# Layer 1 of a two-layer trunk: attention of each head interleaved with the input projection of the next

## What is computed

```python
def _diff_attn(q, k, v, lam):
    ...
        s = jnp.einsum("bqhmd,bnhmd->bhmqn", qi, k2).astype(jnp.float32) * scale
        p = jax.nn.softmax(s, axis=-1)
        amap = p[:, :, 0] - lam * p[:, :, 1]
        return jnp.einsum("bhqn,bnhe->bqhe", amap.astype(v.dtype), v)

def _mixer_c(h, j, l, W, rope, cache):
    q, k, v = jnp.split(h @ W["w_in_c"][j], 3, axis=-1)
    ...
        keys = jnp.concatenate([k_ctx, _rope_pairs(k, rope)], axis=1)
        vals = jnp.concatenate([v_ctx, v], axis=1)
        o = _diff_attn(_rope_pairs(q, rope), keys, vals, lam)
    of = o.astype(jnp.float32)
    of = of * lax.rsqrt(jnp.mean(of * of, axis=-1, keepdims=True) + SUBLN_EPS) * W["c_subln"][j] * (1.0 - lam_init)
    out = of.astype(h.dtype).reshape(bn, t, C_HEADS * C_VDIM) @ W["w_out_c"][j]
    return out, (k, v)
```

## Time and profile before

| | us |
|---|---|
| median of 3 runs | 4068.52 |
| span of the profiled execution | 4070.0 |
| layer 1, input projection (2917.6 to 3089.3) | 171.7 |
| layer 1, attention (3089.3 to 3488.5) | 399.2 |
| layer 1, output projection (3488.5 to 3547.1) | 58.6 |

### The profile page before, as it was taken

One profiled execution on the slowest core, in us unless ns is written; L12 is line 12 of the kernel. 1 busy time (PEld: TensorE's weight loads), 2 busy tenths in 40 slices (PEclk: granted clock), 3 DMA queues, 4 the chain that ended last, 5 costly groups with the idle time before them and its releaser, 6 DMA issues.

```text
span 4070.0 us, 55614 instructions
## 1 busy us (share of the span) xinstructions
PE 3540.9 (87%) x22346; PEld 3286.8 (81%) x22346; DVE 1839.3 (45%) x2902; ACT 998.3 (25%) x1729; POOL 0.2 (0%) x4
## 2 busy tenths in 40 slices
PE   7899998875979797978999989999897555799998
PEld 7899998854868686868999989999895222699997
DVE  2554545443454544445545455554413555332223
ACT  1212122232121212122121232112323444232212
POOL 0000000000000000000000000000000000000000
PEclk6899999965877776879999999999998666899999
DMA  6344441100000000022444424343220000122221
GB/s 193 89 119 119 119 115 56 29 0 19 1 4 1 4 1 2 1 58 60 121 114 114 124 83 117 106 127 110 78 72 7 5 5 25 52 64 81 72 73 57
DMA packets 393639, 264.46 MB, mean 65 GB/s; under 512 B 11627, under 2 KB 375430, under 8 KB 393222
## 3 DMA queue, kind: packets, MB, share of 16 engines
q1 hardware_dynamic: 393478, 262.23, 22.8%
HBM read 258.13 MB, written 4.06 MB: 64 GB/s over the span
## 4 chain that ended last, share of the span: by engine, by line
PE 83%; DVE 10%; ACT 3%; issue 3%; DMA 1%; SPq 0%; DVEq 0%; ACTq 0%
PE pair L1960 56%; PE pair L761 5%; PE pair L1946 2%; PE pair L1274 1%; PE pair L1969 1%; PE pair L1926 1%; DVE big L1780 1%; PE pair L721 1%; PE pair L799 1%; PE pair L722 1%; PE pair L756 1%; PE pair L802 1%; PE pair L1269 1%; DVE w_lo_as_f L1383 1%; PE pair L421 1%
## 5 line engine op out<-in xcount | busy, mean ns | idle before, releaser
L1960 PE MATMUL pair<-h_hi,w_hi 128*128 128x320 f32 x3792 | 875.7, 312 | 120.3 <-DVE h_lo L1789 68.1
L1960 PE MATMUL pair<-h_lo,w_hi 128*128 128x320 f32 x3792 | 873.1, 312 | 0.0
L1960 PE MATMUL pair<-h_hi,w_lo 128*128 128x320 f32 x3792 | 872.3, 312 | 0.0
L1960 PEld LDWEIGHTS pair<-h_hi,w_hi 128*128 128x128 f32 x3792 | 642.1, 190 | 124.1 <-issue 124.1
L1960 PEld LDWEIGHTS pair<-h_lo,w_hi 128*128 128x128 f32 x3792 | 642.8, 190 | 0.0
L1960 PEld LDWEIGHTS pair<-h_hi,w_lo 128*128 128x128 f32 x3792 | 641.7, 190 | 0.0
L1960 PE MATMUL pair<-big_as_f32r,w_hi 128*128 128x320 f32 x2816 | 538.8, 314 | 4.6 <-DVE w_lo L1679 4.4
L1569 ACT ACTIVATE w_hi<-raw 128x1024 fp32r<-128x1024 f32 x333 | 341.3, 1052 | 630.9 <-PE pair L1960 333.0
L1679 DVE TENSOR_TENSOR w_lo<-raw,w_hi 128x1024 fp32r<-128x1024 f32 x333 | 397.5, 1216 | 163.5 <-ACT w_hi L1569 162.7
L1960 PEld LDWEIGHTS pair<-big_as_f32r,w_hi 128*128 128x128 f32 x2816 | 451.3, 192 | 5.6 <-DVE w_lo L1679 5.2
L1824 DVE TENSOR_TENSOR work<-work,pair 128x640 f32<-128x640 f32 x88 | 72.2, 821 | 644.0 <-PE pair L1960 644.0
(11 more groups left out here) (345 smaller groups left out, 3571.1 us busy)
## 6 DMA issues: line engine op xcount, KB each, us to landing
raw<-ffn_w SPq DMA_DIRECT2D x272, 512.0 KB, 5.0
work<-mod_w SPq DMA_DIRECT2D x136, 512.0 KB, 3.8
raw<-w_in_c SPq DMA_DIRECT2D x24, 512.0 KB, 3.8
raw<-w_in_ab SPq DMA_DIRECT2D x21, 512.0 KB, 3.9
w_hi_as_f<-mod_w SPq DMA_DIRECT2D x8, 512.0 KB, 4.7
raw<-w_out_ab SPq DMA_DIRECT2D x8, 512.0 KB, 5.4
raw<-w_out_c SPq DMA_DIRECT2D x8, 512.0 KB, 5.1
h_hi_as_f<-x_sample SPq DMA_DIRECT2D x1, 2048.0 KB
```

Source lines behind the costliest of these rows:

```text
L1960: ins = nc.tensor.matmul(ps[:, c, 0:HALF], w, v[:, k, c * HALF:(c + 1) * HALF], start=(k == 0 and w is hi and v is xh), stop=(k == kts - 1 ...
```

## The change

Projection and attention of layer 1 become one hand-ordered stage, written out head by head without a loop. The columns of the weight matrix are taken head by head (queries, keys, values of head 0, then of head 1, and so on). Three tiles are projected ahead; then PE runs, for each head, the steps of its attention with the three projection tiles of the next head between them, each in two halves. The weighing and the mean squares of a head run inside the next head. All projection tiles go through one PSUM pair (3); scores of the two halves take pairs 0 and 1, one block at a time; everything else (rotations, transposes, keys, values, weighing, mean squares) takes pair 2. The scratch of the attention moves to `big` behind the tiles of two heads, to `work` and to a part of `attn`, so the weight rings and the projection's input stay in use. Maxima, exponentials and sums run over 640 keys in one instruction instead of 512 and 128; the prompt's 128 keys go with block 0. The transfers of cached keys and values and of the prompt's rows go from SP's queue to POOL's. The last head splits the finished output tiles between its own steps, and the weight splits run ahead into the output projection.

The core of the diff (the helpers of ACT and DVE not shown keep their operations):

```diff
-            return i + 1 < len(stages) and stages[i + 1][0] != "out"
+            return i + 1 < len(stages) and stages[i + 1][:2] != ("out", 0)
...
+        def c_tile(h, kind):
+            return big[:, 8 + 3 * (h % 2) + kind, :]
+        CB = 14 * TOK
+        c_keys, c_q = R[:, CB:CB + 640], R[:, CB + 640:CB + 1152]
+        c_vtok = R[:, CB + 1152:CB + 1792].rearrange("p (c n) -> p c n", n=P)
+        c_t2 = R[:, CB + 1792:CB + 2816].rearrange("p (a n) -> p a n", a=2)
+        c_o, c_sq, c_rs = (R[:, CB + 2816 + 640 * i:CB + 3456 + 640 * i] for i in range(3))
+        c_kout, c_kpast, c_vpast, c_ap = (R[:, CB + 4736 + P * i:CB + 4736 + P * (i + 1)] for i in range(4))
...
+        c_e = work[:, 0:2560].rearrange("p (q m n) -> p q m n", q=2, m=2)
+        c_at = work[:, 2560:5120].rearrange("p (i n) -> p i n", i=5)
+        c_a = [attn[:, 1664:2304], work[:, 5248:5888]]
+        C_SPARE, C_PROJ = 2, 3
...
+        def pool_attn_c(pool):
+            kc, vc = T["cache_c_k"][0, 0], T["cache_c_v"][0, 0]
+            pool.wait_ge(n_lo, DT * norm_before["in", 1, 0, 0] + DT)
             for i, name in enumerate(("c_lq1", "c_lq2", "c_lk1", "c_lk2")):
+                pool.dma_start(c_lq[:, i, :], T[name].to_broadcast([P, HD])).then_inc(c_lam, 16)
+            pool.dma_start(c_kpast, kc[:, 0, :]).then_inc(c_load, 16)
+            def keys_out(h):
+                pool.wait_ge(c_act, CAC.value(f"kt_{h}"))
+                pool.dma_start(T["new_c_k"][0, 0][:, h, :], c_kout).then_inc(c_outk, 16)
+                if h + 1 < CH:
+                    pool.dma_start(c_kpast, kc[:, h + 1, :]).then_inc(c_load, 16)
+            keys_out(0)
+            for h in range(CH):
+                if h:
+                    pool.wait_ge(c_pe, CPE.value(f"pv_{h - 1}"))
+                pool.dma_start(c_vpast, vc[:, h, :]).then_inc(c_loadv, 16)
+                if h + 1 < CH:
+                    keys_out(h + 1)
+                pool.wait_ge(c_act, CAC.value(f"vt_{h}"))
+                pool.dma_start(T["new_c_v"][0, 0][:, h, :], c_vtok[:, 4, :]).then_inc(c_outv, 16)
...
+        def pe_attn_c(pe, products):
...
+            def project(j, first=True, last=True):
+                if first:
+                    pe.wait_ge(lo_full, IN_C + j + 1 + RING)
+                    pe.wait_ge(pair_free, IN_C + j + RING)
+                for k in range(0 if first else DT // 2, DT if last else DT // 2):
+                    if j == 0:
+                        pe.wait_ge(n_lo, DT * norm_before["in", 1, 0, 0] + k + 1)
+                    ins = products(pp[C_PROJ], (IN_C + j) % RING, k, h_hi, h_lo, k == 0, k == DT - 1)
+                if last:
+                    ins.then_inc(slab_used, 1)
...
+            def scores(h, b):
+                if b == 0:
+                    pe.wait_ge(c_dve, CDV.value(f"r2_{h}"))
+                    pe.wait_ge(c_act, CAC.value(f"kt_{h}"))
+                    if h:
+                        pe.wait_ge(c_act, CAC.value(f"ex3_{h - 1}"))
+                else:
+                    pe.wait_ge(c_act, CAC.value(f"ex{b - 1}_{h}"))
+                for k0, k1 in ((0, 512), (512, 640)):
+                    for m in range(2):
+                        r = slice(m * HD, m * HD + HD)
+                        ins = nc.tensor.matmul(flat[m][:, k0:k1], c_q[r, b * P:(b + 1) * P], c_keys[r, k0:k1], start=True, stop=True)
+                if b == 0:
+                    for m in range(2):
+                        r = slice(m * HD, m * HD + HD)
+                        ins = nc.tensor.matmul(flat[m][:, 640:768], c_tile(h, 0)[r, LAT:TOK], c_tile(h, 1)[r, LAT:TOK],
+                                               start=True, stop=True)
+                ins.then_inc(CPE.sem(f"sc{b}_{h}"), 1)
+            def turn(h, b):
+                pe.wait_ge(c_dve, CDV.value(f"A{b}_{h}"))
+                if b == 0 and h:
+                    pe.wait_ge(c_act, CAC.value(f"o_{h - 1}"))
+                elif b == 1:
+                    pe.wait_ge(c_act, CAC.value(f"rt_{h - 1}" if h else f"at0_{h}"))
+                elif b == 2:
+                    pe.wait_ge(c_act, CAC.value(f"vt_{h}"))
+                elif b == 3:
+                    pe.wait_ge(c_act, CAC.value(f"at2_{h}"))
+                if b == 0:
+                    nc.tensor.transpose(flat[C_SPARE][:, 640:768], c_ap, ident)
+                for i in range(5):
+                    ins = nc.tensor.transpose(flat[C_SPARE][:, i * P:(i + 1) * P], c_a[b % 2][:, i * P:(i + 1) * P], ident)
+                ins.then_inc(CPE.sem(f"tr{b}_{h}"), 1)
...
+            for j in range(3):
+                project(j)
+            rotate(0)
+            turn_keys(0)
+            scores(0, 0)
+            for h in range(CH):
+                more = h + 1 < CH
+                j = 3 * h + 3
+                if more:
+                    project(j, last=False)
+                if h:
+                    turn(h - 1, 3)
+                if more:
+                    project(j, first=False)
+                if h:
+                    weigh(h - 1)
+                scores(h, 1)
+                turn(h, 0)
+                if more:
+                    project(j + 1, last=False)
+                if h:
+                    mean_squares(h - 1)
+                if more:
+                    project(j + 1, first=False)
+                scores(h, 2)
+                turn(h, 1)
+                if more:
+                    project(j + 2, last=False)
+                    rotate(h + 1)
+                scores(h, 3)
+                if more:
+                    project(j + 2, first=False)
+                    turn_keys(h + 1)
+                turn_values(h)
+                if more:
+                    scores(h + 1, 0)
+                turn(h, 2)
+            turn(CH - 1, 3)
+            weigh(CH - 1)
+            mean_squares(CH - 1)
...
+        def act_attn_c(act, split_hi):
...
+            keys(0)
+            for h in range(CH):
+                more = h + 1 < CH
+                j = 3 * h + 3
+                exps(h, 0)
+                if more:
+                    split_hi(0, IN_C + j + 2)
+                if h:
+                    turned(h - 1, 3)
+                if more:
+                    evict(j)
+                if h:
+                    outputs(h - 1)
+                turned(h, 0)
+                exps(h, 1)
+                if more:
+                    split_hi(0, IN_C + j + 3)
+                if h:
+                    roots(h - 1)
+                if more:
+                    evict(j + 1)
+                else:
+                    split(0)
+                    split(1)
+                turned(h, 1)
+                exps(h, 2)
+                if more:
+                    split_hi(0, IN_C + j + 4)
+                else:
+                    split(2)
+                    split(3)
+                exps(h, 3)
+                if more:
+                    evict(j + 2)
+                    keys(h + 1)
+                values(h)
+                turned(h, 2)
+            split(4)
+            split(5)
+            turned(CH - 1, 3)
+            outputs(CH - 1)
+            split(6)
+            roots(CH - 1)
+            act.wait_ge(c_outk, 16 * CH)
+            act.wait_ge(c_outv, 16 * CH)
+            split(7)
...
+        def dve_attn_c(dve, split_lo):
...
+            def mapped(h, b):
+                u = c_unit(b)
+                parts = [(c_e[:, b % 2], b + 1, c_a[b % 2])] + ([(c_ep, 0, c_ap)] if b == 0 else [])
+                dve.wait_ge(c_act, CAC.value(f"ex{b}_{h}"))
+                v.reciprocal(c_rd[:, u, :], c_den[:, u, :]).then_inc(CDV.sem(f"rd{b}_{h}"), 1)
+                own(f"rd{b}_{h}")
+                v.tensor_scalar(c_l1[:, u, :], c_rd[:, u, 1:2], nlam, None, ALU.mult).then_inc(CDV.sem(f"lm{b}_{h}"), 1)
+                own(f"lm{b}_{h}")
+                for e, i, _ in parts:
+                    ins = v.tensor_scalar(e[:, 1, :], e[:, 1, :], c_l1[:, i, :], None, ALU.mult)
+                ins.then_inc(CDV.sem(f"tm{b}_{h}"), 1)
+                own(f"tm{b}_{h}")
+                if b == 0 and h:
+                    dve.wait_ge(c_pe, CPE.value(f"tr2_{h - 1}"))
+                for e, i, out in parts:
+                    ins = v.scalar_tensor_tensor(out=out, in0=e[:, 0, :], scalar=c_rd[:, i, 0:1], in1=e[:, 1, :],
+                                                 op0=ALU.mult, op1=ALU.add)
+                ins.then_inc(CDV.sem(f"A{b}_{h}"), 1)
...
+            turned_halves(0)
+            rotated(0)
+            maxima(0, 0)
+            for h in range(CH):
+                more = h + 1 < CH
+                j = 3 * h + 3
+                if more:
+                    split_lo(0, IN_C + j + 2)
+                mapped(h, 0)
+                maxima(h, 1)
+                mapped(h, 1)
+                if h:
+                    finish(h - 1)
+                if more:
+                    split_lo(0, IN_C + j + 3)
+                else:
+                    split(0)
+                    split(1)
```

(53 more changed lines are left out.)

472 lines of the change are left out of this document (178 added, 294 removed).

## The result

The changed kernel takes 3863.82 us (median; 3859.69 to 3864.17) against 4069.72 us (4064.79 to 4077.47) of the kernel before in the runs shown with it: a ratio of 0.9489, 95% interval 0.9472 to 0.9506, so 206 us less. The forecast was 3884 us, in a range of 3838 to 3940. The profiled execution spans 3862.0 us.

A forecast was written before the change was run, and what follows sets the result against it. The prediction took a chain over PE, DVE and ACT, no single engine, to bound the attention. Overlapping the projection saved 187.5 us and POOL cost 3: 4068.5 - 187.5 + 3 = 3884 us, range 3838 to 3940.

The forecast's parts named there:

- The walk: One steady head followed through all in-order engine queues: 41.7 us at full clock, PE waiting 3.4 before the next first scores.
- The clock: PE's half-clock stretch after each steady head's idle wait: 2.5 us charged per head, bounds 0 and 5, making 44.2.
- falls once per head: Predicted sign in the steady heads: PE's granted clock drops once in each head; 2.5 us was charged for it.
- prologue to head 0's first scores: Start of layer 1's projection: warm-up 3.0 us, three tiles 21.1, then rotation, sine product, sums and first scores.
- POOL's 3 us: Allowance for the whole kernel for issuing four transfers per head from POOL's queue: 3 us, taken near the lower bound 0.
- The projection's single PSUM pair costs nothing: Claim from the steady head: ACT empties the pair at 9.0, 23.9 and 39.5 us, before the next tile starts.
- (a): Rival: PE runs at half clock through the interleaved heads, 76.5 us a head, 4113 us in all; chance 0.05.
- (b): Rival: new waits for copies from the shared PSUM pair, 7.7 us a head, 54 in all, 3938 us; chance 0.13.
- POOL's upper bound: Every transfer from POOL's queue holds DVE as long as a landing: 8 us per head, 3940 us.
- (c): Rival: no overlap, projection halves only add to the attention, 68 us a head, 4051 us; chance 0.03.
- (d): Rival: no clock loss and no waits in the heads, 37.7 us a head, 3838 us; chance 0.07.

The follow-up runs named there:

- the sequence: Changed kernel with the next head's three projection tiles run back to back after the transposes of block 2, not spread through the head: 4078.6 us, ratio 1.0024.
- whole tiles: Changed kernel with each projection tile run in one piece where its first half stood, instead of in two halves: 3906.39 us, ratio 0.9599.
- less PE work: Changed kernel with only two of eight groups of matmuls run per projection tile from the fourth tile on: 3857.72 us, ratio 0.9479.
- the early half tile: Changed kernel with the next head's first half projection tile moved ahead of its first scores, two ACT steps reordered: 3858.41 us, measured again 3853.30.
- without the reciprocal: Changed kernel with the reciprocal in each head's finish run over one column instead of 640: 3845.44 us, ratio 0.9449.
- changed, again: The changed kernel itself, unaltered, measured later on the same chip as the repeated half-tile versions: 3867.05 us, ratio 0.9503.
- SP's queue: Changed kernel with transfers of cached keys and values and the prompt's rows issued from SP, between weight slabs, instead of POOL: 3869.44 us, ratio 0.9510.
- splits don't run ahead: Changed kernel with the output projection's first two weight slabs split only after the attention, as before the change: 3875.81 us, ratio 0.9517.

## Why the prediction was right, and where it was off

**What bounds the kernel** (a chain over three engines, not one of them) is shown from both sides: without the interleaving nothing is gained, and with it 111 us less of PE work are worth 6 to 9, while 4 us a head less on DVE's part of the chain are worth 18 (3845.44).

**The walk** named the places. After the mean squares the path leaves PE for the root, the reciprocal and two blocks of softmax; the longest wait of a head stands before the next first scores, ended by ACT's key copies or DVE's keys. The rows show 2.7 us there instead of 3.4. Its length at full clock was 41.7 us, and heads in which the clock holds take 40.42. The steps: from the end of the first scores to the reciprocal 20.67 us (3103.47 to 3124.14) against 20.95; from there to the next scores 18.18 against 18.9 + 0.25, where the maxima of a block take 1.66 with their negation (1.48 + 0.18) instead of 1.98, twice on the chain; the scores 1.57 against 1.6. The interpolated size of a maximum wasn't at fault (0.82, measured 817 ns): two of them overlapped are 1.56, and the other 0.42 of the 1.98 was for a negation that takes 0.17. The same kind of walk, made again after the result from the changed kernel's trace, gave 71 for the sequence with falls of the clock (71.8), 47.6 for whole tiles (47.05), 38.9 to 40.9 with less PE work (40.21), 38.6 for the early half tile (39.05) and 38.9 without the reciprocal (38.87).

**The clock** is the term that was mis-sized. I charged 2.5 us to every head. Four profiles have this order in their steady heads (of the run without run-ahead the first four heads); us from head to head:

| profile | steady heads |
|---|---|
| changed | 40.43, 41.89, 40.42, 43.29, 42.05 |
| changed, again | 40.43, 41.78, 40.42, 40.42, 41.91 |
| SP's queue | 40.42, 41.78, 40.42, 40.42, 41.89 |
| splits don't run ahead | 41.99, 41.96, 40.43, 43.30 |

A head without a fall takes 40.42 us, and 10 of the 19 have one, at 1.4 to 2.9 us; the mean over all 19 is 0.9, by profile 0.6 to 1.5. The wait ahead is the same 2.73 us whether the clock falls or not. That the clock "falls once per head" was wrong. The second head falls and the third holds in all four profiles, so it is hardly scatter alone; what decides is open. That the falls hang on the wait is shown: where work fills it the clock is 1.00 in all 15 steady heads of three profiles, and where it is cut to 1.3 us (no reciprocal) in all five.

**The sum by its terms**, forecast and measured: prologue to head 0's first scores 31.6 and 33.3; head 0 33.8 and 33.5; six heads 265.2 and 249.7; last head 52 and 49.9; output projection with its wait 59.1 and 59.0. Fifteen of the 20 us that the forecast was too high lie in the six heads (some 8 in the walk, 8 in the clock). The stages ahead let the projection begin 3.9 us earlier, which is luck, and POOL's 3 us, which no row had stood for, were not there; against that stand 3.3 us between the profiled execution's place beside its median before (1.5 above it in span) and after (1.8 below). Two slips in the working change nothing: six heads of 44.2 from 2983.0 on end at 3248.2, not 3248.5, and the middle heads of before are 46.1 to 47.8 us apart (mean squares to mean squares), where the earlier trace rows shows only one of them.

**"The projection's single PSUM pair costs nothing"** held in the heads and failed in the prologue, where the three tiles follow one another: the second and the third wait 0.9 us each for the eviction (the row with 1.8, 2, 0.9). That is about the prologue's excess. The walk had been made for a steady head only.

**POOL.** The four issues of a head are short, here two of them and DVE's scaling beside the first:

```profile
3102.09 0.64 POOL L1174 DMA_DIRECT2D new_c_k<-big  x1 [25.42 <-ACT big L1328]
3102.72 0.53 POOL L1176 DMA_DIRECT2D big<-cache_c_k  x1
```

```profile
3102.06 0.55 DVE L1453 TENSOR_SCALAR work<-work,big 128x640 f32<-128x640 f32 x1
```

The scaling takes the 0.55 us that it took with POOL idle. The Trainium skill (SBUF — State Buffer, Who interferes with whom) says that VectorE and GpSimd can block one another at a shared port pair, and names `tensor_scalar` among the operations that can take it. The lock itself can't be seen in this trace; if it was taken here, it left nothing in the time, since five heads with POOL's queue and with SP's take the same 204.95 us.

**The rivals.** (a) half clock throughout: the clock is 0.94 to 1.00 in the heads with a projection beside them. (b) waits for copies out of the shared pair: 3.0 + 2.6 + 1.8 us and two single ones of 1.1 and 0.8, 9.3 in the whole layer, not 54; POOL's upper bound: nothing, as above. (c) sums instead of overlap: that is the kernel in sequence, 71.8 us a head. (d) neither clock loss nor waits, 37.7 us a head: the measured time lies 26 us above it and 20 below the forecast, so it was nearly as close; the early half tile comes within 1.4 us a head of it.

## What to carry to other kernels

Where one stage is dense on an engine and the next is a chain over three, lay the one into the other in pieces of the size of the chain's links, and walk the in-order queues with durations from the trace: the walk gave the length of a head to 1.3 us before the result (clock-free heads), and to about a microsecond for the variants once the changed kernel's own trace was there. Walk the first round as well as the steady one. Then look for the one wait that is left and put a piece of the dense work exactly there: filling 2.7 us also kept the clock up, so 11 us of the layer came from moving half a tile and two steps of ACT. An engine that is 90% busy need not be the bound; take its work away once and see.

## What the runs showed of the hardware

- The granted clock answered the same wait of 2.73 us in a stream of about 40 us of dense work with a fall in 10 of 19 heads, not always and not never; a fall cost 1.4 to 2.9 us. The scores behind the wait then took up to 2.50 us instead of 1.35 (1.2 against 2.4 GHz).
- Two maxima of 640 elements straight from PSUM take 1.48 to 1.57 us together on the chain, 0.82 each (817 ns mean), as the line between the 256 and the 1024 elements of the earlier trace rows gives.
- A reciprocal of 128 x 640 takes 4.15 us, as before, over four times the scaling and the combining (0.55 and 0.88) of the same tile. No other single DVE instruction on the chain of a head is as long.
